# One decode and prefill step of a hybrid recurrent trunk: the first norm moved behind the first products, wider seam parts, weight splits moved to GpSimd

## The reference

```python
for l in range(2):
    hn = rms_norm(x, norm_mix_pre[l])
    mix = even_mixer(hn) if l == 0 else odd_mixer(hn)   # projection in, recurrences, projection out
    x = x + rms_norm(mix, norm_mix_post[l])
    hn = rms_norm(x, norm_ffn_pre[l])
    x = x + rms_norm(swiglu(hn, w_ffn_in[l], w_ffn_out[l]), norm_ffn_post[l])

def rms_norm(x, w):
    return x * rsqrt(mean(x * x, axis=-1) + 1e-6) * w
```

## Time and profile before

| | us |
|---|---|
| median of 3 runs (lowest, highest) | 3597.11 (3594.98, 3597.2) |
| the profiled execution | 3592.51, its span 3590.5 |
| TensorE busy | 3327.2 (93%) |
| VectorE, GpSimd, ScalarE busy | 1935.1 (54%), 1521.7 (42%), 1206.9 (34%) |
| mean granted TensorE clock | 0.961 of 2.4 GHz |

### The profile page before, as it was taken

The page is one execution under the profiler, slowest core; times in us unless marked ns, Lnnn a source line. Parts: engine busy times, 40 slices in busy tenths (PEclk is TensorE's granted clock), DMA queues, the critical chain, the costliest instruction groups (busy, mean ns, idle before and its releaser), DMA issues.

```text
span 3590.5 us, 63459 instructions
## 1 busy us (share of the span) xinstructions
PE 3327.2 (93%) x24606; PEld 3208.1 (89%) x24606; DVE 1935.1 (54%) x2539; ACT 1206.9 (34%) x1496; POOL 1521.7 (42%) x888
## 2 busy tenths in 40 slices
PE   7899997868789999999999899997979999999997
PEld 7899985747779999999999799985979999999997
DVE  3544546574786443244446778646784442344466
ACT  3443543231333332233332334432233332333322
POOL 4444652000344444544443436642444445444443
PEclk9999997879899999999999999998999999999999
DMA  5333432000434444444444264444434444444443
GB/s 168 118 131 124 136 131 74 3 26 4 141 109 140 149 152 151 148 139 148 152 153 153 96 212 129 160 147 194 152 101 151 147 153 150 136 152 147 158 148 110
DMA packets 118673, 475.00 MB, mean 132 GB/s; under 512 B 13425, under 2 KB 15089, under 8 KB 115569
## 3 DMA queue, kind: packets, MB, share of 16 engines
q1 hardware_dynamic: 108864, 421.58, 36.5%
q10 hardware_dynamic: 9648, 51.17, 3.7%
HBM read 450.66 MB, written 22.03 MB: 132 GB/s over the span
## 4 chain that ended last, share of the span: by engine, by line
PE 85%; DVE 9%; ACT 3%; issue 2%; POOL 0%; ACTq 0%; DMA 0%; DVEq 0%; POOLq 0%
PE ps L330 48%; PE ps L334 25%; DVE w_lo L306 1%; DVE x_lo L599 1%; PE ps L357 1%; ACT w_hi L295 1%; PE ps L362 1%; PE ps L1066 1%; PE ps L2023 1%; PE ps L1546 1%; PE ps L1088 1%; PE ps L1510 0%; PE ps L1548 0%; PE ps L1495 0%; PE ps L1720 0%
## 5 line engine op out<-in xcount | busy, mean ns | idle before, releaser
L306 POOL TENSOR_TENSOR w_lo<-raw,w_hi 128x512 fp32r<-128x512 f32 (+2 forms) x756 | 1390.9, 1841 | 1801.4 <-ACT w_hi L295 1795.5
L330 PE MATMUL ps<-x_hi,w_hi 128*128 128x320 f32 x4832 | 1441.9, 312 | 14.2 <-ACT w_hi L295 7.1
L330 PE MATMUL ps<-x_lo,w_hi 128*128 128x320 f32 x4832 | 1432.4, 310 | 0.0
L295 ACT ACTIVATE w_hi<-raw 128x1024 fp32r<-128x1024 f32 (+1 forms) x756 | 840.5, 1112 | 1636.7 <-PE ps L334 1541.4
L306 DVE TENSOR_TENSOR w_lo<-raw,w_hi 128x512 fp32r<-128x512 f32 (+2 forms) x692 | 631.4, 914 | 698.2 <-ACT w_hi L295 687.2
L330 PEld LDWEIGHTS ps<-x_hi,w_hi 128*128 128x128 f32 x4832 | 912.5, 189 | 23.3 <-ACT w_hi L295 12.7
L330 PEld LDWEIGHTS ps<-x_lo,w_hi 128*128 128x128 f32 x4832 | 912.2, 189 | 0.8
L334 PE MATMUL ps<-x_hi,w_lo 128*128 128x320 f32 x4832 | 811.2, 310 | 25.0 <-DVE w_lo L306 23.4
L334 PEld LDWEIGHTS ps<-x_hi,w_lo 128*128 128x128 f32 x4832 | 734.7, 188 | 31.2 <-POOL w_lo L306 19.3
L330 PE MATMUL ps<-u_hi,w_hi 128*128 128x320 f32 x1408 | 417.7, 311 | 8.3 <-DVE u_lo L711 8.3
L330 PE MATMUL ps<-u_lo,w_hi 128*128 128x320 f32 x1408 | 417.3, 310 | 0.0
(11 more groups left out here) (402 smaller groups left out, 2771.7 us busy)
## 6 DMA issues: line engine op xcount, KB each, us to landing
raw<-in_w_ffn_in SPq DMA_DIRECT2D x352, 512.0 KB, 3.5
raw<-in_w_ffn_out SPq DMA_DIRECT2D x128, 704.0 KB, 4.0
raw<-in_w_in_even SPq DMA_DIRECT2D x116, 512.0 KB, 3.5
raw<-in_w_in_odd SPq DMA_DIRECT2D x96, 512.0 KB, 3.5
raw<-in_w_out_even SPq DMA_DIRECT2D x32, 512.0 KB, 3.5
raw<-in_w_out_odd SPq DMA_DIRECT2D x32, 512.0 KB, 3.5
hS<-in_state_hgrn ACTq DMA_DIRECT2D x4, 1024.0 KB, 5.6
out_hgrn_s<-hS ACTq DMA_DIRECT2D x4, 1024.0 KB, 4.3
```

The source lines that it names most:

```text
L295: nc.scalar.activation(w_hi[s % 2][:, 0:g.kt, :], raw[s % 4][:, 0:g.kt, :], ACT.Copy)\
L306: eng.tensor_tensor(w_lo[s % 2][:, k0:k1, :], raw[s % 4][:, k0:k1, :], w_hi[s % 2][:, k0:k1, :].bitcast(f32), sub).then_inc(sem(f"split_lo ...
L330: nc.tensor.matmul(out, w_hi[s % 2][:, k, :], x[:, kk, :], start=half == 0 and k == 0 and x is xh, stop=False)
```

## The change

First, the start. `pre_norm_*` goes. ScalarE makes `x_hi` from X·w without the norm factor, VectorE `x_lo`; the units of `in_a` multiply these at once, and VectorE multiplies the eight tiles by `srow` = 1/rms as it evacuates them. The mean square is summed by VectorE from ScalarE's squares and by one matmul of ones ahead of unit 7. Beside units 10 to 13 VectorE makes the normalised slices `xs_even`, and ScalarE and VectorE split these again for `in_b`. The norm vectors are loaded ahead of X, and three constants of the even mixer later, behind unit 14's split.

Second, the seams: five parts of 2, 2, 4, 4 and 4 slices; VectorE multiplies and adds, ScalarE writes `yw` (X' times the next weight) and then `x_hi` from it, and VectorE subtracts one from the other. GpSimd's `seam_pool` goes.

Third, `in_b` gets `lo_dve` 0, so that `fill_dve` goes. TensorE's first transposes of an HGRN group wait for the previous group's `pse` (a step of ScalarE's) instead of its end.

Fourth, `multiply_head` takes the first two slices unit by unit and waits for each unit's `w_hi` by itself.

```diff
-        dense("in_b", d["w_in_even"], EVEN_TILES - FIRST_TILES, KU_MODEL, 2, FIRST_TILES)
+        dense("in_b", d["w_in_even"], EVEN_TILES - FIRST_TILES, KU_MODEL, 0, FIRST_TILES)
...
             for half in range(2):
                 units = (g.unit0 + 2 * half, g.unit0 + 2 * half + 1)
+                for t, s in enumerate(units):
+                    pe.wait_ge(sem("split_hi"), s + 1)
                     for x in (xh, xl):
+                        products(s, t, half, 0, x)
+                for k in range(2, g.kt, 2):
+                    for x in (xh, xl):
                         for t, s in enumerate(units):
+                            products(s, t, half, k, x)
...
+        def first_act(act):
+            g = plan["in_a"]
+            act.wait_ge(sem("vecs_in"), 16)
             for c in range(8):
                 act.wait_ge(sem(f"x_in{c}"), 16)
+                for k in (2 * c, 2 * c + 1):
+                    ins = act.activation(x_hi[:, k, :], X[:, k, :], ACT.Copy, scale=vec("mix_pre", k))
+                ins.then_inc(sem("x_hi"), 1)
+                if c in (5, 6):
+                    split_hi(act, 0, g.unit0 + c - 3)
+            for c in range(8):
                 act.activation(part(sq, c), part(X, c), ACT.Square).then_inc(sem("norm_sq"), 1)
+            for s in range(g.unit0 + 4, g.unit0 + g.units):
+                split_hi(act, 0, s)
+                if s == g.unit0 + 7:
+                    act.wait_ge(sem("norm_ms"), MS[0])
+                    act.activation(srow, PS[7][:, 0:T], ACT.Sqrt, bias=rms_eps, scale=1.0 / D_MODEL)
+                if s == g.unit0 + 14:
+                    act.wait_ge(sem("xn"), 8)
+                    for dst, src in ((hgm_in[:, :, :], "hgm"), (evc[:, :], "evc"), (sh_in[:, :, :], "shift_in")):
+                        act.dma_start(dst, d[src]).then_inc(sem("even_consts"), 16)
...
+        def first_dve(dve):
             for c in range(8):
+                dve.wait_ge(sem("x_hi"), c + 1)
                 for k in (2 * c, 2 * c + 1):
+                    ins = dve.scalar_tensor_tensor(x_lo[:, k, :], X[:, k, :], vec("mix_pre", k),
+                                                   x_hi[:, k, :].bitcast(f32), mult, sub)
+                if c == 6:
+                    split_lo(dve, "dve", 0, g.unit0 + 2)
+            split_lo(dve, "dve", 0, g.unit0 + 3)
+            L(dve.tensor_tensor(sq[:, 0:4, :], sq[:, 0:4, :], sq[:, 4:8, :], add))
+            split_lo(dve, "dve", 0, g.unit0 + 4)
...
+            for s in (5, 6, 7):
+                split_lo(dve, "dve", 0, g.unit0 + s)
+            dve.wait_ge(sem("norm_rms"), MS[0])
+            L(dve.reciprocal(srow, srow))
...
+            for n in range(8, g.units):
+                split_lo(dve, "dve", 0, g.unit0 + n)
+                if n == 8:
+                    tile(5)
+                tile(n - 1)
+                if 10 <= n < 14:
+                    for c in (2 * (n - 10), 2 * (n - 10) + 1):
+                        for k in (2 * c, 2 * c + 1):
+                            ins = dve.scalar_tensor_tensor(xs_even[:, k, :], X[:, k, :], vec("mix_pre", k), srow,
+                                                           mult, mult)
+                        ins.then_inc(sem("xn"), 1)
+            for c in (0, 1):
+                x_lo_part(dve, part(xs_even, c), c, FILL["in_b"])
+            tile(g.units - 1)
+            for c in range(2, 8):
+                x_lo_part(dve, part(xs_even, c), c, FILL["in_b"])
...
+        SEAM_PARTS = ((0, 1), (1, 2), (2, 4), (4, 6), (6, 8))
...
+            for q, (c0, c1) in enumerate(SEAM_PARTS):                       # seam_act
+                act.wait_ge(sem("seam_y"), NPARTS * b + q + 1)
+                for k in range(2 * c0, 2 * c1):
+                    dst = x_hi[:, k, :] if q == 0 else yw[:, k, :]
+                    ins = act.activation(dst, X[:, k, :], ACT.Copy, scale=vec(w[0], KT * w[1] + k))
...
+                act.activation(span(x_hi, c0, c1), span(yw, c0, c1), ACT.Copy)\
+                   .then_inc(sem("x_hi"), c1 - c0)
+                if q == 3:
+                    split_hi(act, 0, g.unit0 + 2)
+                    split_hi(act, 0, g.unit0 + 3)
+            for c in range(0, 8, 2):
+                act.activation(span(M, c, c + 2), span(X, c, c + 2), ACT.Square).then_inc(sem("norm_sq"), 1)
...
-        def seam_pool(pool, n, g):
...
+            def grow(q):                                                    # seam_dve
+                c0, c1 = SEAM_PARTS[q]
+                x = span(X, c0, c1)
+                L(dve.tensor_tensor(x, x, bc(stat[:, 1, :].unsqueeze(1), P, 2 * (c1 - c0), T), mult))
+                dve.tensor_tensor(x, x, span(M, c0, c1), add).then_inc(sem("seam_y"), 1)
+            def low(q):
+                c0, c1 = SEAM_PARTS[q]
+                dve.wait_ge(sem("x_hi"), 8 * fill + c1)
...
+                    ins = dve.tensor_tensor(span(x_lo, c0, c1), span(yw, c0, c1),
+                                            span(x_hi, c0, c1).bitcast(f32), sub)
...
             split_hi(act, 0, g.unit0)                                       # fill_act
+            act.wait_ge(sem("xn"), 8)
+            act.wait_ge(sem("unit_done"), g.unit0 - 1)
+            for c in range(4):
+                act.activation(part(x_hi, c), part(xs_even, c), ACT.Copy).then_inc(sem("x_hi"), 1)
...
+                if u == 0:
+                    act.wait_ge(sem("unit_done"), g.unit0)
+                    for c in range(4, 8):
+                        act.activation(part(x_hi, c), part(xs_even, c), ACT.Copy).then_inc(sem("x_hi"), 1)
...
-        def fill_dve(dve):
...
                 if g:
-                    pe.wait_ge(sem("hgrn_end"), g)
+                    hgrn_wait(pe, "pse", g - 1)
...
+            for g in range(HGROUPS):
+                by_stage(hgrn_dve(dve, g))
+            dve.wait_ge(sem("hgrn_end"), HGROUPS)
+            pass_over(dve, plan["in_b"])
```

More of the change, by code:

```diff
@@ L338, in multiply_head, with products @@
         def multiply_head(pe, g, xh, xl, fill):
+            outs = [PS[(g.tile0 + t) % 4][:, 0:T] for t in range(2)]
+            def products(s, t, half, k, x):
+                kk = half * g.kt + k
+                if x is xh:
+                    pe.wait_ge(sem("x_hi"), 8 * fill + kk // 2 + 1)
+                else:
+                    x_lo_wait(pe, fill, kk // 2)
+                for a in range(2):
+                    nc.tensor.matmul(outs[t], w_hi[s % 2][:, k + a, :], x[:, kk + a, :],
+                                     start=kk + a == 0 and x is xh, stop=False)
+            if g.tile0:
+                pe.wait_ge(sem("tile_out"), g.tile0)
             for half in range(2):
                 units = (g.unit0 + 2 * half, g.unit0 + 2 * half + 1)
[L343 to L349, removed]
+                for t, s in enumerate(units):
+                    pe.wait_ge(sem("split_hi"), s + 1)
                     for x in (xh, xl):
[L351 to L354, removed]
+                        products(s, t, half, 0, x)
+                for k in range(2, g.kt, 2):
+                    for x in (xh, xl):
                         for t, s in enumerate(units):
-                            for a in (k, k + 1):
-                                nc.tensor.matmul(outs[t], w_hi[s % 2][:, a, :], x[:, half * g.kt + a, :],
-                                                 start=half == 0 and a == 0 and x is xh, stop=False)
+                            products(s, t, half, k, x)
                 for t, s in enumerate(units):
@@ L630, in seam_sum_pe @@
         def seam_sum_pe(pe, n):
-            pe.wait_ge(sem("seam_dve"), 3 * SEAM[n] + 2)
+            if n == 0:
+                pe.wait_ge(sem("first_sum"), 1)
+                nc.tensor.matmul(PS[7][:, 0:T], ones, sq[:, 0, :], start=True, stop=True).then_inc(sem("norm_ms"), 1)
+                return
+            pe.wait_ge(sem("seam_dve"), 2 * SEAM[n] + 1)
             nc.tensor.matmul(PS[7][:, 0:T], ones, M[:, 0, :], start=True, stop=True).then_inc(sem("norm_ms"), 1)
@@ L818, in fill_act @@
                     act.activation(sh_out[:, n, :], ps[:, 255:T:8], ACT.Copy).then_inc(sem("tile_out"), 1)
-        def fill_dve(dve):
-            g = plan["in_b"]
-            for u in range(g.units):
-                yield fill_stage(u)
-                split_lo(dve, "dve", 0, g.unit0 + u)
         def fill_pe(pe):
@@ L829, in fill_pe @@
                 yield fill_stage(u)
-                multiply_unit(pe, 0, g.unit0 + u, x_hi, x_lo)
+                multiply_unit(pe, 0, g.unit0 + u, x_hi, x_lo, FILL["in_b"])
         def hgrn_act(act):
@@ L2209, in _ @@
             pe.wait_ge(sem("com_in"), 16)
-            pre_norm_pe(pe, 0)
-            multiply(pe, plan["in_a"], x_hi, x_lo, FILL[0])
+            multiply(pe, plan["in_a"], x_hi, x_lo, FILL[0], 0)
             by_stage(fill_pe(pe), hgrn_pe(pe))
```

156 lines of the change are left out of this document (60 added, 96 removed).

## The result

| | before | after |
|---|---|---|
| median, us (lowest, highest) | 3596.05 (3594.88, 3597.2), 4 runs | 3554.54 (3553.91, 3557.81), 4 runs |
| ratio of after to before, 95% interval | | 0.9886 [0.9869, 0.9904] |
| the profiled execution (span) | 3592.51 (3590.5) | 3554.26 (3552.4) |

The account below looks back on a forecast made before the run. TensorE was taken as the bound (85% of the chain), so only its standstills and low clock pay. -14.4 + 3 - 13 - 13.5 = -37.9 gave 3554.6, or 3559 us on the median's footing; range 3544 to 3574.

Parts of the forecast that it names:

- A: Start, deferred norm: unit 4 starts at 33.2 instead of 48.44 us, +0.8 later in these tiles; -14.4 us in all.
- Later in these tiles: Start, after unit 4 begins: ones matmul and wait for first evacuation add 0.8 us; normalised slices cost zero.
- B: Boundary from `in_a` to `in_b`: splitting X a second time costs +3 us, bounds +2 to +5.7.
- C: `in_b` beside HGRN: GpSimd alone splits low parts, so waits for VectorE's pieces go; -13 us, bounds 0 and -22.
- R1: Rival: GpSimd replaces VectorE as the late splitter in `in_b`, so C is 0; 3572 us, chance 0.12.
- R3: Rival, slower: contention stretches GpSimd's pieces beside HGRN until they pace `in_b`; 3648 us at 5.0 per piece; chance 0.04.
- -18.6: Gain within C, in us, before adding 5.6 of new waits for GpSimd's and ScalarE's parts.
- D: Three seams: VectorE's work falls from 30 to 20 us, ScalarE becomes the chain; -4.5 us each, -13.5 together.
- R2: Rival: ScalarE bounds the seams with copies, two splits and squares in one queue, so D is 0; 3573 us, chance 0.10.
- the marks: Two marks on VectorE after HGRN: no TensorE wait stands on them, so zero.

Follow-up runs that it names:

- experiment 5: Kernel after with GpSimd's wait for the shift constants moved from ahead of its first `in_b` piece to behind its fifth; 3554.15 us.
- experiments 2 to 4: Kernel after with VectorE again splitting two, one and four of eight slices of each `in_b` unit; 3579.6, 3586.81 and 3565.73 us respectively.
- Experiment 6: Kernel after with the adds of seam parts 1 to 4 done by GpSimd again instead of VectorE; 3563.22 us.
- experiment 7: Kernel after with eight narrow seam parts of two slices instead of five of 2, 2, 4, 4, 4; 3542.27 us.
- experiment 8: Kernel after with two edits undone: heads take slice pairs for both units, HGRN transposes wait for `hgrn_end` again; 3557.8 us.
- experiment 1: Kernel after with VectorE's sums of squares taken apart and put behind the splits of units 5 and 6; 3538.45 us.

## Why the prediction was right, point by point

**A, the start: right until unit 4, then short.** Unit 4 began at 31.31 (forecast 33.2); ScalarE's squares were done at 30.2, not 32.1. In all A is -10.75 instead of -14.4. The step that failed is "Later in these tiles": I costed ones matmul, evacuation and normalised slices, but not the adds over the squares that the diff puts before the split of unit 5. They cost TensorE the wait of 2.74 us. Another 2.7 is the low clock behind that wait in the profiled execution; in experiment 5's trace A would be -13.5.

**B, the boundary: right.** +3.4 for +3. As forecast, ScalarE's HGRN block and the split of unit 19 behind it end the stretch (that split is done at 100.16). GpSimd's first piece began 6.26 us after the end of `in_a` (forecast 6.2) and ended TensorE's wait of 5.5:

```profile
88.68 2.50 PE L334 MATMUL ps<-x_hi,w_lo 128*128 128x320 f32 x8 [5.54 <-POOL w_lo L306]
```

**C, `in_b`: right in kind, too small.** -23.1 for -13, just past its lower bound of -22. GpSimd's new waits were sized rightly (1.8 for 2). Two parts were not. I added 3.6 for ScalarE's parts, as TensorE would meet its blocks sooner; these waits fell from 7.1 to 3.8. And the clock: TensorE's idle time fell by 16.3 us (22.2 to 5.9), its busy time for the same matmuls by 6.8 (445.4 to 438.7). That low-clock time stood only in my bound and belongs in the sum, though its size is no fixed share of the waits: against the kernel after, `in_b` with one slice has 23.3 us more of idle time and 13.5 more of busy time, with four slices 11.5 and 1.0.

```profile
95.97:577.23 481.26, 452.15 (x2894) 427.69 (x2893) 256.32 (x416) 205.96 (x309) 251.30 (x172) 0.96 0.38 125
```

```profile
97.37:554.41 457.04, 439.65 (x2894) 415.88 (x2893) 245.68 (x412) 203.97 (x308) 189.09 (x172) 0.99 0.40 132
```

The pieces took 2.51 us (2.57 forecast), so R1 and R3 fall. Two figures of mine were off without changing that: -18.6 held 0.3 us of waits for GpSimd that the earlier trace rows don't show, and R3 took GpSimd's old pieces at 1.85 us where they averaged 1.99.

As for the shared port, the Trainium skill (SBUF — State Buffer, "Who interferes with whom") says that the port pair which both use is an exclusive lock, and that a VectorE instruction with two SBUF inputs contends with a GpSimd instruction that reads SBUF. By that rule, the trace agrees: 1.96 us for a piece of 0.28 beside one of 2.12. I used it against the change (HGRN's products may stand 0.7 us longer per unit), and that came true. The weight pieces were 70.33 of VectorE's 247.82 us in `in_b` before:

```profile
107.41:575.00 467.59, 132.46 (x776) 118.40 (x776) 70.33 (x97) 193.43 (x97) 0.97 0.39 129
```

The other 312 instructions took 177.5 us; after, the same 312 take 234.9, which is 0.6 more per unit. But no wait of TensorE in `in_b` is for one of them. What I left out is the other side, which experiments 2 to 4 show: in the old kernel it was VectorE's late weight piece that stood, and TensorE waited for that.

**D, the seams: right until unit 4, then given back.** Unit 4's low product comes 5.4 us sooner from the seam's begin (34.3 instead of 39.65; forecast 4.5, with `x_hi` ending the waits as forecast). Then the sums of squares, three adds of which GpSimd made before, take 4.3 back: net -1.05, where D had -4.5. The step that failed is "the four wide sums (4.3) stand between splits 4 and 5 on VectorE, up to 1.5 late". The sums are there, but that term is too small: they take 7.4 us, as the two wide adds take 5.10 beside GpSimd's splits, and TensorE waits 2.74 and runs its next eight matmuls in 2.47 instead of 1.34. Experiment 6 confirms that the seams' adds of M belong on VectorE, experiment 7 that the wider parts were a loss. R2 names the right engine only for part of it: ScalarE ends waits of about 1.2 us in each half, VectorE the 2.74 behind.

**What I counted as nothing** (the `pse` wait, the marks, the order in the heads): not contradicted, and not settled below 3 us. The time behind `in_b` until TensorE's first matmul after HGRN fell by 1.9 us, but 1.6 of these are the sixteen matmuls at another granted clock in experiment 8's windows.

**The sum.** -10.75 + 3.4 - 23.1 - 1.9 - 3 x 1.05 = -35.5 of the 38.1. Another 3 lie in two stretches that the change doesn't touch, the first units of two `down` products, 1.5 each: at the first, the kernel before ran 36 us with a granted clock of 0.95, after with 1.00.

```profile
1364.00:1400.00 36.00, 33.93 (x221) 33.66 (x221) 13.19 (x18) 10.44 (x9) 15.24 (x9) 0.95 0.49 168
```

```profile
1330.00:1366.00 36.00, 33.93 (x232) 33.67 (x231) 13.28 (x19) 10.44 (x9) 16.77 (x9) 1.00 0.51 174
```

So that the total came out within 0.2 us is luck. The sums of squares (left out of A, too small in D) and the low clock at the start took back 14 of A and D; C brought 10 more than forecast, and nearly 5 came from stretches that no term has, most of it by a higher granted clock. With the sums behind the splits, as experiment 1 shows, the kernel is at 3538, below the forecast's range.

## What to carry to other kernels

When work leaves one engine, ask which engine inherits it and what stands behind it there: four adds in front of one weight split, made longer by GpSimd's splits beside them, ate most of what a well-built seam had gained (4.3 of 5.4 us). Give the engine that works in the order of the consumer the whole of a small job rather than sharing it with one that has a program of its own; and before parts are widened, compare the two sizes per element, since at equal cost the narrower part reaches the consumer sooner (in experiment 7 the low products of the first half began 3.7 us sooner in the first seam).

## What the runs showed of the hardware

A two-input piece of VectorE's that begins while a GpSimd instruction runs can't be made cheap in this kernel by making it small: 256 elements took 0.73 us on average and 128 took 0.69, because the GpSimd instruction that it meets sets the end (0.14 us behind it for 128 elements, 0.28 for 256). And the clock blurs a few microseconds: the same matmuls of `in_b` were busy between 438.7 and 443.4 us at a granted clock of 0.98 or 0.97, with waits that differ by 1 us at most, and after the same wait of 2.7 us eight matmuls took 1.40 or 2.47 us. So an edit worth 1.5 us has to be judged in its own stretch, and by more than one execution.
